# A mixture of 32 experts on one core: the second expert's gate and up products directly behind the first's, in a bank of their own, and the gathering's halves around the first down products

## What is computed

```python
def run_block(args):
    xb, e = args
    hid = jax.nn.silu(xb @ w_gate[e]) * (xb @ w_up[e])
    return hid @ w_down[e]
```

## Time and profile before

| | |
|---|---|
| Time, median of 3 runs | 943.96 us (943.73 to 944.25) |
| Profiled execution: its own time | 943.72 us |
| Profiled execution: span from first to last instruction | 941.7 us |
| TensorE busy | 909.7 us, 97% of the span |
| VectorE, ScalarE, GpSimd busy | 278.6, 208.4, 198.1 us |
| Mean granted clock of TensorE | 0.998 of full speed |
| Bytes moved by DMA | 286.12 MB, mean 304 GB/s |
| DMA rate in the slices from 210 to 610 us | 412 to 431 GB/s, nearly all of them 425 to 430 |
| DMA rate in the slices from 118 to 188 us | 299, 189 and 337 GB/s |

### The profile page before, as it was taken

The page is one execution under the profiler, slowest core; times in us unless marked ns, Lnnn a source line. Parts: engine busy times, 40 slices in busy tenths (PEclk is TensorE's granted clock), DMA queues, the critical chain, the costliest instruction groups (busy, mean ns, idle before and its releaser), DMA issues.

```text
span 941.7 us, 13189 instructions
## 1 busy us (share of the span) xinstructions
PE 909.7 (97%) x5196; PEld 536.3 (57%) x5196; DVE 278.6 (30%) x734; ACT 208.4 (22%) x498; POOL 198.1 (21%) x329
## 2 busy tenths in 40 slices
PE   7999999999999999999989899999999999999996
PEld 5788687544434444344434344488766558688544
DVE  3399824320011101011001011134136346250334
ACT  3355624211001111011101011132215511011640
POOL 0188400111111111111111011031003202013221
PEclk9999999999999999999999999999999999999999
DMA  9999974899999999999999999993400943202001
GB/s 361 425 425 399 407 299 189 337 381 430 428 428 427 428 425 429 426 429 427 429 427 429 427 426 421 429 412 135 164 2 13 421 171 122 90 11 80 1 1 45
DMA packets 23962, 286.12 MB, mean 304 GB/s; under 512 B 2658, under 2 KB 3426, under 8 KB 5090
## 3 DMA queue, kind: packets, MB, share of 16 engines
q1 hardware_dynamic: 23184, 283.99, 72.8%
q10 hardware_dynamic: 722, 1.33, 0.4%
HBM read 284.26 MB, written 1.05 MB: 303 GB/s over the span
## 4 chain that ended last, share of the span: by engine, by line
PE 75%; DMA 16%; DVE 6%; issue 1%; ACT 1%; SPq 0%; POOL 0%; POOLq 0%; DVEq 0%
PE bank L1020 18%; PE bank L1267 17%; DMA arena<-in_w_expert_up 10%; PE bank L1284 9%; PE bank L1488 5%; DVE bank L1740 5%; PE bank L1294 4%; DMA arena<-in_w_expert_down 3%; PE bank L1435 3%; DMA arena<-in_w_ada 3%; PE bank L1467 2%; PE bank L1255 2%; PE bank L1501 1%; PE bank L1626 1%; PE bank L1452 1%; PE bank L1513 1%
## 5 line engine op out<-in xcount | busy, mean ns | idle before, releaser
L1267 PE MATMUL bank<-arena 128*64 128x512 f32 x1024 | 226.2, 593 | 11.3 <-DMA arena<-in_w_expert_up 11.1
L1020 PE MATMUL bank<-arena 128*128 128x256 f32 (+1 forms) x992 | 211.1, 373 | 0.6 <-ACT arena L871 0.4
L1020 PEld LDWEIGHTS bank<-arena 128*128 128x128 f32 x992 | 183.2, 190 | 27.1 <-issue 3.4
L1267 PEld LDWEIGHTS bank<-arena 128*64 128x64 f32 x1024 | 76.2, 137 | 156.1 <-issue 155.0
L1284 PE MATMUL bank<-arena 128*64 128x512 f32 x512 | 116.9, 598 | 1.2 <-DVE arena L1933 0.6
L841 ACT ACTIVATE arena<-bank 128x512 f32<-128x512 f32 x32 | 19.1, 598 | 376.4 <-PE bank L1276 376.4
L1937 DVE TENSOR_TENSOR arena<-bank,arena 64x512 f32<-64x512 f32 x32 | 21.8, 682 | 264.1 <-ACT arena L837 264.1
L599 POOL COPY der<-arena 128x4 f32 (+1 forms) x30 | 5.6, 187 | 318.8 <-PE bank L1276 299.1
L1284 PEld LDWEIGHTS bank<-arena 128*64 128x64 f32 x512 | 33.9, 136 | 67.2 <-issue 64.7
L1294 PE MATMUL bank<-arena 64*128 64x256 f32 x512 | 65.8, 386 | 0.6 <-DVE arena L1955 0.5
L1740 DVE SCALAR_TENSOR_TENSOR bank<-arena,par,bank 128x256 f32<-128x256 f32 x143 | 58.3, 485 | 0.6
(11 more groups left out here) (259 smaller groups left out, 844.4 us busy)
## 6 DMA issues: line engine op xcount, KB each, us to landing
arena<-in_w_expert_down SPq DMA_DIRECT2D x29, 2048.0 KB, 31.4
arena<-in_w_expert_up SPq DMA_DIRECT2D x28, 2048.0 KB, 27.1
arena<-in_w_expert_gate SPq DMA_DIRECT2D x27, 2048.0 KB, 28.8
arena<-in_w_ada SPq DMA_DIRECT2D x12, 2048.0 KB, 34.7
arena<-in_w_expert_gate SPq DMA_DIRECT2D x10, 1024.0 KB, 32.0
arena<-in_w_expert_up SPq DMA_DIRECT2D x8, 1024.0 KB, 33.1
arena<-in_w_kv SPq DMA_DIRECT2D x4, 2048.0 KB, 10.3
arena<-in_w_in_b SPq DMA_DIRECT2D x4, 2048.0 KB, 15.3
```

The lines of the kernel that those rows point to most:

```text
L1020: mm = pe.matmul(bank[part:part + m, at:at + n], w[:, k, lo:lo + m], rhs[:, k0 + k, :], start=(i == 0), stop=(i == tiles - 1))
L1267: mm = pe.matmul(GU_BANK[half * WIN:(half + 1) * WIN, :], xw[b][:, k, :], w[:, k, :], start=(k == 0), stop=(k == KD - 1), skip_group_check ...
```

## The change

- The gathering's tiles use banks 4 to 7 alone, in both halves.
- TensorE's order at the beginning is now begin(0), begin(1), turn(0), gather(0), finish(1) with the down products of expert 0, gather(1), begin(2), finish(2).
- begin(1) writes bank 2 (`SECOND_GU`), and so waits for that bank's readers and no longer for `hidden_ready`, which stands before turn(0) instead. It still waits for `window_ready` to reach 2.
- ScalarE and VectorE take their steps in the order that follows from it: expert 1's `silu` and `gated` ahead of the gathering's reads, and expert 0's down result between the two halves.
- `JOIN` is 15: the extra slot takes up 5 and no longer gate 5. Gate 5 goes to the slot of down 0.
- GpSimd's program is not edited.

```diff
-EXTRA, JOIN = RING, 14
+EXTRA, JOIN = RING, 15
...
-                plan(("gather", half, j), (7, 1, 2, 4, 5, 6, 7, 1)[j] if half else 1 + (j + 5) % 7)
+                plan(("gather", half, j), 4 + j % 4)
...
+        SECOND_GU = ps[2]
...
             silu(gu_full, 1, silu_done)
+            move_turned(t_full, C_T + 1, 0, t_moved)
+            silu(gu_full, 2, silu_done, SECOND_GU)
             for j in range(0, KD, 2):
                 gathered(0, j)
-            move_turned(t_full, C_T + 1, 0, t_moved)
-            silu(gu_full, 2, silu_done)
...
                 if not first:
                     pe.wait_ge(win_ready, e + 1)
-                    pe.wait_ge(hid_ready, e)
+                    if e == 1:
+                        pe.wait_ge(sem("bank2_read"), BEFORE_EXPERTS[2])
+                    else:
+                        pe.wait_ge(hid_ready, e)
+                bank = SECOND_GU if e == 1 else GU_BANK
...
-            for e in range(FIRST):
-                begin(e, e % BODY, first=e == 0)
-                if e == 1:
-                    pe.wait_ge(sem("bank3_read"), BEFORE_EXPERTS[3])
-                    turn(0).then_inc(t_full, 1)
-                if e < 2:
-                    gather(e)
-                if e:
-                    for b in range(1, 4) if e == 1 else range(4, 8):
-                        pe.wait_ge(sem(f"bank{b}_read"), BEFORE_EXPERTS[b])
-                    finish(e, e % BODY, second=e == 1, third=e == 2)
+            begin(0, 0, first=True)
+            begin(1, 1)
+            pe.wait_ge(sem("bank3_read"), BEFORE_EXPERTS[3])
+            pe.wait_ge(hid_ready, 1)
+            turn(0).then_inc(t_full, 1)
+            gather(0)
+            pe.wait_ge(sem("bank1_read"), BEFORE_EXPERTS[1])
+            finish(1, 1, second=True)
+            gather(1)
+            begin(2, 0)
+            for b in range(4, 8):
+                pe.wait_ge(sem(f"bank{b}_read"), BEFORE_EXPERTS[b])
+            finish(2, 0, third=True)
...
             dve.wait_ge(silu_done, 1)
             gated(hid_ready)
-            for half in range(2):
-                for j in range(1, KD, 2):
-                    gathered(half, j)
-            with dve.Fori(1, EXPERTS) as e:
+            dve.wait_ge(silu_done, 2)
+            gated(hid_ready, SECOND_GU)
+            for j in range(1, KD, 2):
+                gathered(0, j)
+            dve.wait_ge(y_full, 1)
+            move_result(y_moved)
+            for j in range(1, KD, 2):
+                gathered(1, j)
+            with dve.Fori(2, EXPERTS) as e:
```

More of the change, by code:

```diff
@@ L833, in gathered, with silu @@
                                bias=mod[:, 24 + j:25 + j], scale=a2[:, j:j + 1]).then_inc(read(name), 1)
-            def silu(full_sem, n, done):
+            def silu(full_sem, n, done, bank=GU_BANK):
                 act.wait_ge(full_sem, n)
-                act.activation(hid, GU_BANK[WIN:2 * WIN, :], ACT.Silu).then_inc(done, 1)
+                act.activation(hid, bank[WIN:2 * WIN, :], ACT.Silu).then_inc(done, 1)
             def move_turned(full_sem, n, b, done):
@@ L1259, in _, with gate_up @@
             pe.wait_ge(sem("bank0_read"), BEFORE_EXPERTS[0])
-            def gate_up(b, wu, wg, ready=None, ks=range(KD)):
+            def gate_up(b, wu, wg, ready=None, ks=range(KD), bank=GU_BANK):
                 for k in ks:
@@ L1266, in gate_up @@
                     for half, w in ((0, wu), (1, wg)):
-                        mm = pe.matmul(GU_BANK[half * WIN:(half + 1) * WIN, :], xw[b][:, k, :], w[:, k, :],
+                        mm = pe.matmul(bank[half * WIN:(half + 1) * WIN, :], xw[b][:, k, :], w[:, k, :],
                                        start=(k == 0), stop=(k == KD - 1), skip_group_check=True)
@@ L1316, in begin @@
                 ready = (lambda k: moved(pe, ("first", k))) if first else None
-                mm = gate_up(b, wu, wg, ready, range(KD // 2))
+                mm = gate_up(b, wu, wg, ready, range(KD // 2), bank)
                 if e < FIRST:
@@ L1327, in begin @@
                         landed_whole((kind, e))
-                gate_up(b, wu, wg, ready, range(KD // 2, KD)).then_inc(gu_full, 1)
+                gate_up(b, wu, wg, ready, range(KD // 2, KD), bank).then_inc(gu_full, 1)
             def finish(e, b, second=False, third=False):
@@ L1934, in gathered, with gated @@
                                   mod[:, 24 + j:25 + j], ALU.mult, ALU.add).then_inc(read(name), 1)
-            def gated(done):
-                dve.tensor_tensor(hid, GU_BANK[0:WIN, :], hid, ALU.mult).then_inc(done, 1)
+            def gated(done, bank=GU_BANK):
+                dve.tensor_tensor(hid, bank[0:WIN, :], hid, ALU.mult).then_inc(done, 1)
             def move_result(done):
```

## The result

| | before | after |
|---|---|---|
| Time, median of 4 runs each | 943.85 us (943.49 to 944.25) | 953.84 us (952.46 to 954.96) |
| Ratio of the times, 95% interval | | 1.0107 (1.0095 to 1.0119) |
| Profiled execution, time and span | 943.72, 941.7 us | 953.97, 951.8 us |
| Mean granted clock | 0.998 | 0.992 |
| TensorE busy | 909.7 us | 913.8 us |

The changed kernel is 10.0 us slower. The forecast was slower by 5.6, at 949.5, with a range up to 953.3; the time is above the range. Two executions of the kernel before, among the 19 timed beside a later set of kernels, took 1579.5 and 1579.7 us at a mean clock of 0.557; the ratios leave them out.

The account below looks back on a forecast made before the run. The weight-transfer stream was taken to bound the kernel. Expert 2's 7.1 us delay, less 1.9 or 0.9 spare, with expert 1's -3.6 us eaten up, gave +5.6: 949.5 us, range 947.8 to 953.3.

Parts of the forecast that it names:

- the clock: TensorE's clock behind the new gaps of 3.4 and 4.2 us: the sum held no fall to 1.2 GHz.
- Expert 1's products: After expert 0: TensorE idles 3.4 us for GpSimd's second selection, then starts at 175.1 instead of 178.71, 3.6 us earlier.
- Banks and readers: In the gathering: the smaller number of banks costs nothing, covered by 2 us.
- Down products: Expert 0's, between the gathering's halves: start at 190.1 instead of 194.30, end at 193.7; the 0.64 us wait goes.
- Expert 2's window: Behind the gathering: lost cover of 3.65 us; expert 2 begins at 205.1 instead of 198.02, 7.1 us later.
- What the stream spares: At down 5's release in the weight stream: 1.9 us to spare by landings, 0.9 by bytes; shift taken as 5.6.
- a rival of 0.25: Ahead of expert 2: the clock falls, adding 3.1 us, for 952.6; chance 0.25.
- a sign of being wrong: Between 205 and 215 us: a granted clock under 1.00 would show the forecast wrong.
- The price per fall: From the kernel's first matmuls: about 6.3 us at half speed, 3.1 us lost per clock fall.
- The faster rival: In the weight stream from 180 to 184: expert 1's earlier pairs are kept, -3.0 us, 941.0; chance 0.05.
- a window that isn't last: Ahead of expert 2: it begins at 200.9 when the second half ends, 2.9 us late, 944.9; chance 0.04.
- a stream that covers more: At expert 2's half pairs and up 6: the queue catches up, shift as low as 4 us, 947.9; chance 0.06.

Follow-up runs that it names:

- half_first_early: Changed kernel with the gathering's first half back between experts 0 and 1, and GpSimd's early selection for expert 2: 944.26 us, ratio 1.0012.
- both_filled: Changed kernel with seven unused matmuls ahead of expert 1's products and nine ahead of expert 2's: 949.12 us, ratio 1.0062.
- late8: Kernel before with eight unused matmuls ahead of expert 2's products: 945.60 us, ratio 1.0020.
- late15: Kernel before with fifteen unused matmuls ahead of expert 2's products: 948.64 us, ratio 1.0049.
- early_window: Changed kernel with GpSimd making expert 2's selection while the gathering runs, only the copy left behind it: 949.86 us, ratio 1.0069.
- tiles_in_gap: Kernel before with expert 1 early, four gathering tiles filling its gap, banks 4 to 7 and GpSimd's early selection: 943.17 us, ratio 0.9991.
- gap2_filled: Changed kernel with nine unused matmuls ahead of expert 2's products alone: 951.20 us, ratio 1.0084.
- gap1_filled: Changed kernel with seven unused matmuls ahead of expert 1's products alone: 951.28 us, ratio 1.0077.
- half_first: Changed kernel with the gathering's first half back between expert 0's and expert 1's products: 950.46 us, ratio 1.0074.
- before_early5: Kernel before with the gathering on banks 4 to 7 and GpSimd's early selection, second timing: 942.88 us, ratio 0.9989.

## Why the prediction was wrong, point by point

The step that failed is the clock: the sum held TensorE at full speed behind both new gaps, and it fell to half in both. The rest of the sum held but for a term of 1.0 us.

- **The bound and the direction** were right. The stream is full to the end in both kernels, and what it loses before 234 us reaches the end.
- **Expert 1's products**: the gap of 3.4 us behind GpSimd's second selection was forecast and measured at 3.42. Their start at 174.93, with expert 0 at 164.43, is the forecast one.
- **Banks and readers** at nothing: nothing else shows (half_first_early is 0.6 us over the kernel before at a delay of 1.6). Down products: forecast 7.2 us after turn, measured 191.51 - 184.40 = 7.1.
- **Expert 2's window** was right: a gap of 4.38 us, 3.65 of it lost cover.
- **What the stream spares** was put too high: 1.9 or 0.9 us forecast, 1.5 taken, and in the kernel after it was 0.5. The forecast let down 5 land 8.0 us after its issue, as into an empty queue, although by its own times up 6 was to land only at 226.5, behind down 5's issue at 225.2; down 5 took 9.6. Of the miss of 4.4 us (10.0 less 5.6) this is 1.0; the other 3.4 are TensorE's delay, 10.5 us instead of 7.1. Without falls of the clock the runs spare 1.9 (both_filled), 1.8 (late8) and 1.7 (late15), so that the term was about right for the case that the forecast took.
- **The clock is the step that failed.** The sum held the clock at full speed and left a fall to a rival of 0.25, for the second gap alone. It fell in both gaps, in every profile of a kernel that has them, and between 205 and 215 it was under 1.00, which the forecast had named as a sign of being wrong. The row that it went by, 4.2 us of idle time at the end of the program, shows that so much was enough once, not that less isn't: 3.4 us were enough three times of three. At that same place in the program the 13 profiles have from 2.1 us of idle time ahead of the fall to 5.3, so one trace could not give a length (the last lines of this document show both). The price per fall, 3.1 us from the first matmuls, was too high for this kernel: 3.4 us at half speed, 1.7 us lost. It was read from the rate of the records, for the granted clock in those rows is 1.00, and it is near what the two long falls cost (2.8 us in early_window, 2.9 in late15). Two falls are 3.4 us of TensorE; in time both together cost 4.7 (after against both_filled), by intervals of 1.1 and 1.6 us not told from 3.4. By the Trainium skill, "TensorE: Matmul & The Clock Gate", section "HAM oscillation — how this bites in real kernels", waits between bursts bring the engine back to half rate; the measurement sides with this rule, at a smaller price for each fall than the forecast had put on it.
- **The faster rival**: its mechanism, early pairs kept for good, is refuted by tiles_in_gap. There expert 2 begins 32.5 us after expert 0 and not 33.4 as before, and the pairs still bring nothing beyond that.
- **The other two rivals**, a window that isn't last and a stream that covers more, did not come: the gap ahead of expert 2 was 4.38 us, and the spare time was under the forecast's, not over it.
- The forecast's sum of 5.2 to 6.2 us is what the kernel costs with both gaps filled (5.2, with an interval of 1.6); the other 4.7 us went when the falls did.

## What to carry to other kernels

Work that stands behind a wait may be the cover for that wait: before moving it forward, look at what the engine would then stand idle for, here 3.65 us of down products that had hidden the making of the next window. A new gap of some microseconds on TensorE can cost more than its length: here each of 3.4 and 4.4 us brought a stretch at half clock, and unused matmuls in the gap kept it away (both_filled). A sum for such a change should hold the fall as a term, and not only as a rival. In this stream with its ring of slots, an early release brought nothing when the next releases were not early too.

## What the runs showed of the hardware

- Gaps of 3.4 us (after, early_window, gap2_filled) and 4.4 us (after, gap1_filled, half_first) had a fall to 1.2 GHz in six cases of six, and gaps of 1.5 us in none of two. The two waits of 3.0 us for a matrix (after, late15) had one each; waits of 1.4 to 2.4 us for a matrix (the longest in late8) none.
- The length of a gap alone does not tell. In before_early5 and gap2_filled the clock also fell at 13.9 and 13.8 us, for 3.4 us each, behind waits of 2.19 and 1.67 us and with the engine busy again. At the end of the program, in the 13 profiles, it fell 2.1 to 5.3 us after the last matmul.
- A fall cost 1.4 to 1.7 us in five of the six gaps and 2.8 us in early_window, by the length of the group behind it (8.48, 8.78 and 9.92 us against 7.09). It may come when the engine is busy again, as at 176 in the kernel after, 1.1 us into the products.
- Starting expert 2 a microsecond earlier brought 1.0 us (before_early5, with an interval from 0.2 to 1.9), though a delay of 3.5 us costs only 1.7.

The end of the program in half_first, whose last matmul ends at 938.59 and whose clock falls at 940.7, and in both_filled, where the last ends at 938.71 and the clock falls at 944.0:

```profile
938.00:939.00 1.00, 0.59 (x3) 0.19 (x1) 0.30 (x1) 0.00 (x0) 0.00 (x0) 1.00 0.00 0
...
940.50:941.00 0.50, 0.00 (x0) 0.00 (x0) 0.50 (x2) 0.37 (x1) 0.00 (x0) 0.70 0.00 0
```

```profile
939.00:944.00 5.00, 0.00 (x0) 0.00 (x0) 3.58 (x7) 0.95 (x2) 2.24 (x2) 1.00 0.01 5
944.00:944.50 0.50, 0.00 (x0) 0.00 (x0) 0.00 (x0) 0.00 (x0) 0.00 (x0) 0.50 1.03 394
```
